# Seven products for eight: the retention values and the first gate by Strassen's scheme

## The chip, the cores and the metric

One core of one Trainium2 chip runs the whole kernel: two blocks of a network on 256 tokens of width 1024, batch 1, all in f32. The metric is the device time of one execution in microseconds. TensorE takes an f32 product as three matmuls of rounded parts, so every weight needs a high and a low part that ScalarE and VectorE make on the fly.

## The reference, cut to what matters

The change lies in the second block, between its first and its second feed-forward layer:

```python
u = rmsnorm(h, norm_mix[l])                       # h: 256 x 1024
proj = u @ w_in[l]
q, k, v, g_ret, p, gates = jnp.split(proj, split_points, axis=-1)
q = rotary(...); k = rotary(...) * (RET_QK_DIM ** -0.5)
ret = retention(q, k, v)                          # scores * inner_decay, then @ v, 4 heads of 256
ret = ret * lax.rsqrt(mean(ret * ret) + NORM_EPS)
ret = ret * jax.nn.silu(g_ret)
pool_out = multiscale_pool(p, pool_w[l], pool_scale[l])
gate = jax.nn.sigmoid(gates.reshape(b, s, 2, D_MODEL) + gate_bias[l])
merged = gate[:, :, 0] * (ret @ w_ret_up[l]) + gate[:, :, 1] * (pool_out @ w_pool_up[l])
h = h + merged @ w_out[l]
```

`v` and the first of the two gates are each a product of u (256 x 1024) with a 1024 x 1024 matrix.

## The kernel before, in words

Five engines run five programs that are written out by hand; each engine executes its list in order, and semaphores join them. A wait stops all that stands behind it on that engine.

**Weights.** They come in units of 1 MB (128 x 2048 f32), one after the other over one DMA queue, into a ring `raw` of four. `hi` (line 206, ScalarE) casts a unit to its high part `whi`, `lo` (line 213, VectorE) writes the rest `wlo`; both rings hold four units as well. `hi` and `lo` of unit v wait until unit v - 4 is used up by TensorE, `lo` waits for `hi`, and the load of unit v waits for `lo` of unit v - 4.

**Products.** `mm3` (line 258) is one f32 product by three matmuls: high x high, high x low, low x high. `quarter` multiplies one half of the input width (j, four slices of 128) for one half of the tokens (t) by one unit: 4 x 3 = 12 matmuls of 512 columns. `chunk` runs the four quarters of 512 output columns, into the PSUM banks 4 and 5. So a unit serves two quarters, 24 matmuls.

**The stage.** TensorE's order in `tensor_ret` (line 2293): pool input p0, p1; second gate g10, g11 with the pool windows between; pool mixing pw; values v0; pool projection pu0, pu1; values v1; q0, k0, q1, k1 with rotation, scores and values of four heads between; retention gate gr0, gr1; first gate g00, g01; retention projection ru0, ru1; output. `scalar_ret` (2393) and `vector_ret` (2464) have the orders of the other two. The names that matter: `vector_gate` (2124) takes a gate out of PSUM with its bias, `scalar_gate` (2136) the sigmoid; `scalar_ret_gate` (2280) empties the banks 4 and 5 of gr0 and gr1 with a SiLU; `vector_ret_norm` (2260) normalises two heads, with two roots on GpSimd in it; `vector_ret_scores` (2224) multiplies scores by the decay mask; `vector_rotary` (2193) rotates q or k; `split_turned_act` / `_dve` (from line 408) make high and low part of a transposed tile; `scalar_pool_out` / `vector_pool_out` (2156, 2164) those of the pool's output. `norm_half_act` (355) and `norm_half_dve` (374) do it for the normalised x of each stage, here the one named `nm`.

## Time and profile before

| | us |
|---|---|
| median of 3 runs | 1196.01 (1195.92 to 1196.31) |
| profiled execution | 1195.67 |
| its span, first to last instruction | 1193.9 |
| TensorE busy (matmul) | 1184.1 |
| VectorE busy | 915.2 |
| ScalarE busy | 674.6 |
| GpSimd busy | 165.2 |

In the profile PE is TensorE's matmuls, PEld its weight loads, which overlap them, DVE is VectorE, ACT is ScalarE, POOL is GpSimd, SP the engine that issues the DMAs. A name such as L218 is a line of the kernel. Many operations go through helpers and so share a line: L218 is `lo`, L211 `hi`, L259 to L261 are the three matmuls of `mm3`, L267 is a transpose.

### The profile page before, as it was taken

The numbers are of one execution on the slowest core, as the hardware profiler recorded it, in microseconds if no ns is written. First come the engines' busy times: TensorE is split into PE (matmuls) and PEld (weight loads), VectorE is DVE, ScalarE is ACT, GpSimd is POOL, SyncE is SP. The second block draws the span as 40 slices with busy tenths as digits, with TensorE's granted clock in tenths as the row PEclk, the third lists the DMA queues.
The fourth block names the chain that finished last, engine by engine and source line by source line (L and its number), as shares of the span: only waits on it lengthen the run. The fifth ranks groups of instructions, "written<-read, shape, count | busy, mean of one in ns | idle before, by whom it ended". The sixth has DMA issues, their size and how long they took to land.

```text
span 1193.9 us, 14696 instructions
## 1 busy us (share of the span) xinstructions
PE 1184.1 (99%) x5728; PEld 982.7 (82%) x5728; DVE 915.2 (77%) x1143; ACT 674.6 (57%) x814; POOL 165.2 (14%) x169
## 2 busy tenths in 40 slices
PE   9999999999999999999999999999999999999997
PEld 8777888888887888888888888888899888888886
DVE  7788898888778798877798878645567666988884
ACT  7775756656646666654666554545333545666552
POOL 2100132210200132210132120000000000222200
PEclk9999999999999999999999999999999999999999
DMA  9434565547333565556455556745544445555540
GB/s 340 177 138 158 183 235 200 183 175 271 129 119 130 187 228 184 187 181 235 149 199 188 182 207 210 281 163 188 201 152 160 158 176 171 189 207 179 189 176 36
DMA packets 32728, 220.91 MB, mean 185 GB/s; under 512 B 3761, under 2 KB 4273, under 8 KB 7058
## 3 DMA queue, kind: packets, MB, share of 16 engines
q1 hardware_dynamic: 32514, 219.77, 51.4%
q8 instruction: 45, 0.74, 0.2%
q14 instruction: 25, 0.20, 0.1%
q10 hardware_dynamic: 144, 0.20, 0.0%
HBM read 218.91 MB, written 1.05 MB: 184 GB/s over the span
## 4 chain that ended last, share of the span: by engine, by line
PE 98%; issue 1%; DVE 1%; ACT 0%; POOL 0%; POOLq 0%; DVEq 0%; ACTq 0%
PE ps L259 30%; PE ps L261 30%; PE ps L260 30%; PE ps L264 5%; PE ps L267 3%; DVE h L406 0%; DVE AR L2579 0%; DVE st L1812 0%; DVE AR L1830 0%; DVE AR L2201 0%; ACT AR L2570 0%; POOLq L134 0%; DVE AR L2202 0%; POOL st L395 0%; POOL state L1546 0%
## 5 line engine op out<-in xcount | busy, mean ns | idle before, releaser
L218 DVE SCALAR_TENSOR_TENSOR wlo<-raw,whi 128x2048 fp32r<-128x2048 f32 x160 | 366.3, 2294 | 116.2 <-ACT whi L211 89.1
L211 ACT CAST whi<-raw 128x2048 fp32r<-128x2048 f32 x162 | 309.9, 1914 | 195.3 <-PE ps L261 193.2
L259 PE MATMUL ps<-whi,xh 128*128 128x512 f32 x1040 | 410.1, 394 | 0.0
L261 PE MATMUL ps<-whi,xl 128*128 128x512 f32 x1040 | 405.4, 390 | 0.0
L260 PE MATMUL ps<-wlo,xh 128*128 128x512 f32 x1040 | 404.9, 389 | 0.0
L259 PEld LDWEIGHTS ps<-whi,xh 128*128 128x128 f32 x1040 | 195.2, 188 | 45.4 <-issue 1.2
L261 PEld LDWEIGHTS ps<-whi,xl 128*128 128x128 f32 x1040 | 195.2, 188 | 42.0
L260 PEld LDWEIGHTS ps<-wlo,xh 128*128 128x128 f32 x1040 | 195.4, 188 | 38.5
L259 PE MATMUL ps<-whi,yh 128*128 128x512 f32 x344 | 137.9, 401 | 0.0
L261 PE MATMUL ps<-whi,yl 128*128 128x512 f32 x344 | 134.4, 391 | 0.0
L260 PE MATMUL ps<-wlo,yh 128*128 128x512 f32 x344 | 134.0, 390 | 0.0
L395 POOL TENSOR_TENSOR st<-st,nhalf 128x1 f32<-128x1 f32 (+3 forms) x28 | 26.8, 959 | 671.4 <-DVE st L386 383.0
L545 ACT ACTIVATE sil<-ps,st 128x256 f32<-128x256 f32 x88 | 42.0, 477 | 123.3 <-PE ps L261 123.3
L243 DVE SCALAR_TENSOR_TENSOR wlo<-raw,whi 128x512 fp32r<-128x512 f32 x152 | 99.4, 697 | 12.5 <-ACT whi L211 11.0
L651 DVE SCALAR_TENSOR_TENSOR hid<-ps,st,sil 128x256 f32<-128x256 f32 x88 | 42.4, 482 | 43.8 <-ACT sil L545 43.8
L261 PEld LDWEIGHTS ps<-whi,yl 128*128 128x128 f32 x344 | 64.6, 188 | 13.7
L831 POOL TENSOR_TENSOR sums<-AR 128x128 f32<-128x128 f32 x32 | 26.7, 836 | 350.4 <-ACT AR L563 350.4
L259 PEld LDWEIGHTS ps<-whi,yh 128*128 128x128 f32 x344 | 64.7, 188 | 12.2 <-issue 0.4
L254 ACT CAST whi<-raw 128x1024 fp32r<-128x1024 f32 x72 | 74.7, 1043 | 0.0
L260 PEld LDWEIGHTS ps<-wlo,yh 128*128 128x128 f32 x344 | 64.8, 188 | 11.8
L836 POOL TENSOR_TENSOR sums<-AR,sums 128x128 f32<-128x128 f32 x32 | 65.0, 2031 | 2.5
L362 ACT ACTIVATE xh<-ps,pr 128x128 fp32r<-128x128 f32 x108 | 29.6, 385 | 47.2 <-PE ps L267 47.2
(256 smaller groups left out, 1381.1 us busy)
## 6 DMA issues: line engine op xcount, KB each, us to landing
raw<-in_w SPq DMA_DIRECT2D x198, 1024.0 KB, 4.8
raw<-in_w SPq DMA_DIRECT2D x4, 512.0 KB, 7.4
h<-in_x SPq DMA_DIRECT2D x4, 256.0 KB, 4.7
raw<-in_w SPq DMA_DIRECT2D x4, 256.0 KB, 4.4
AR<-in_b_pw SPq DMA_DIRECT2D x1, 1024.0 KB, 4.8
AR<-in_gate_bias SPq DMA_DIRECT2D x1, 1024.0 KB, 7.0
AR<-in_dft SPq DMA_DIRECT2D x1, 864.0 KB, 7.7
AR<-in_rmask SPq DMA_DIRECT2D x1, 768.0 KB, 8.9
```

Of the source, the lines that this page charges most:

```text
L211: e.copy(whi[:, v % S, :], raw[:, v % R, :]).then_inc(*sig.up("hi", v))
L218: e.scalar_tensor_tensor(out=wlo[:, v % S, :], in0=raw[:, v % R, :], scalar=1.0, in1=whi[:, v % S, :].bitcast(F32), op0=ALU.mult, op1=ALU. ...
L243: e.scalar_tensor_tensor(out=wlo[:, v % S, cols], in0=raw[:, v % R, cols], scalar=1.0, in1=whi[:, v % S, cols].bitcast(F32), op0=ALU.mult, ...
L254: e.copy(whi[:, v % S, cols], raw[:, v % R, cols]).then_inc(*sig.up("hi", v) if k else sig.up("hi_half", v))
L259: e.matmul(o, ah, bh, start=start, stop=False, skip_group_check=skip)
L260: e.matmul(o, ah, bl, start=False, stop=False, skip_group_check=skip)
L261: return e.matmul(o, al, bh, start=False, stop=stop, skip_group_check=skip)
L264: return e.matmul(o, a, b, start=start, stop=stop, skip_group_check=skip)
L267: return e.transpose(o, i, ident[0:i.shape[0], 0:i.shape[0]])
L545: e.activation(sil[:, t, :], ps[banks.of[key, t]][:, 0:256], ACT.Silu, bias=0.0, scale=rstd[:, t:t + 1]).then_inc(*sig.up("sil", f, j, t))
L651: e.scalar_tensor_tensor(out=hid[:, t, :], in0=ps[b][:, 256:512], scalar=scale, in1=sil[:, t, :], op0=ALU.mult, op1=ALU.mult).then_inc(*ba ...
L836: e.tensor_tensor(s4, a12, s2, ALU.subtract).then_inc(*sig.up("sums", f, j))
```

## The change

Both `v` and the first gate are computed as one group each, in place of two chunks. The input is cut into four blocks (two token halves x two width halves), the weight matrix into four of 512 x 512 by width half and output half: b11, b21, b12, b22, each a unit. Seven block products of 12 matmuls, four on sums of weight blocks, give the result, where the eight quarters were. In detail:

- `tensor_product` runs product p = 0 to 6 of a group with weight unit v + p, each unit for one product. Products 0, 2 and 5 take x itself, the other four take sums of x blocks (`sxh`, `sxl`) that are made once for both groups. The order in TensorE's queue: v0 and v1 become one group between pw and pu0, so v1 moves ahead of pu0, pu1. The group g0 stands where g00, g01 stood, with the transposes of the second half after products 1 and 2.
- Four of the seven units are sums of weight blocks. `vector_group_sum` makes each in place in the `raw` ring, 128x2048 f32 on VectorE: sum 1 (b11 + b12) after `lo` of unit v, sum 6 (b12 + b22), sum 4 (b22 + sum 1) after `lo` of v + 3, sum 5 (b21 + sum 4) after `lo` of v + 2. `hi` of these units waits for the sum. A group is loaded as four units and split as seven, so the loads of later units wait for the last user of a buffer.
- The result is put together by `scalar_part` (four copies out of PSUM, scaled, on ScalarE) and `vector_part` (four scaled additions on VectorE). The first gate's bias is added by four `vector_gate_sum`.
- The banks of a group are 4, 5 and 6 for v, 4, 5 and 2 for g0. The second product takes bank 5.
- x of this stage is kept in f32 (`x32`): ScalarE writes x32 out of PSUM, copies it to the high part, VectorE subtracts. Four sums on VectorE, one copy on ScalarE and one subtraction give `sxh`, `sxl`.
- `vector_ret_scores` of heads 0 and 1 moves ahead of the rotation of q1's first half and the `lo` behind it.
- The size of a scratch area for DMA descriptors is set to 8192.

```diff
@@ -26,7 +26,11 @@
+         "ffa": 33, "ret": 47, "ffb": 33}
+RET = {"p0": 2, "p1": 2, "g10": 2, "g11": 2, "pw": 1, "v": 7, "pu0": 2, "pu1": 2, "q0": 2, "k0": 2, "q1": 2, "k1": 2,
+       "gr0": 2, "gr1": 2, "g0": 7, "ru0": 2, "ru1": 2, "out": 4}
+GROUPS = ("v", "g0")
+GROUP_RAW = (0, 0, 2, 1, 1, 2, 3)
...
+        raw_of, n = [], 0
+        while len(raw_of) < NU:
+            if len(raw_of) in (RU[g] for g in GROUPS):
+                raw_of += [n + k for k in GROUP_RAW]
+                n += 4
+            else:
+                raw_of.append(n)
+                n += 1
+        users = {}
+        for v, n in enumerate(raw_of):
+            users.setdefault(n, []).append(v)
+        sums_at = {RU[g] + k: RU[g] for g in GROUPS for k in (1, 4, 5, 6)}
...
+            if name == "nm":
+                b = banks.of["x", name, t, half]
+                q.wait_ge(*sig.at("sums", "n1", FAST - 1))
+                q.wait_ge(*sig.at("turned_lo", "n1", FAST - 1))
+                for i in range(4):
+                    k = 4 * half + i
+                    last = e.activation(x32[:, t, k, :], ps[b][:, 128 * i:128 * i + 128], ACT.Copy, bias=0.0,
+                                        scale=parm(name, k))
+                last.then_inc(*banks.empty("x", name, t, half))
+                q.wait_ge(*banks.emptied("x", name, t, half))
+                if x_free:
+                    q.wait_ge(*x_free)
+                e.copy(xh[:, 4 * half:4 * half + 4, tcols(t)],
+                       x32[:, t, 4 * half:4 * half + 4, :]).then_inc(*sig.up("xh", name, t, half))
+                return
...
+            if name == "nm":
+                at = (slice(None), slice(4 * half, 4 * half + 4), tcols(t))
+                e.tensor_tensor(xl[at], x32[:, t, 4 * half:4 * half + 4, :], xh[at].bitcast(F32),
+                                ALU.subtract).then_inc(*sig.up("x_low", t, half))
+                return
...
+        GBANK = {"v": (4, 5, 6), "g0": (4, 5, 2), "g1": (4, 5, 2)}
+        DONE = {(0, 0): "y0", (0, 1): "z", (1, 0): "y1", (1, 1): "x"}
...
+        def vector_group_sum(e, q, g, k):
+            v = RU[g]
+            b11, b21, b22, b12 = (raw_at(v + i) for i in (0, 2, 3, 6))
+            if k == 1:
+                q.wait_ge(*lo_at(v))
+                q.wait_ge(*sig.at("raw%d" % (raw_of[v + 6] % R), raw_of[v + 6]))
+                d = e.tensor_tensor(b11, b11, b12, ALU.add)
+            elif k == 6:
+                q.wait_ge(*sig.at("summed", v + 1))
+                q.wait_ge(*sig.at("raw%d" % (raw_of[v + 3] % R), raw_of[v + 3]))
+                d = e.tensor_tensor(b12, b12, b22, ALU.add)
+            elif k == 4:
+                q.wait_ge(*lo_at(v + 3))
+                q.wait_ge(*sig.at("summed", v + 6))
+                d = e.tensor_tensor(b22, b22, b11, ALU.add)
+            else:
+                q.wait_ge(*lo_at(v + 2))
+                q.wait_ge(*sig.at("summed", v + 4))
+                d = e.tensor_tensor(b21, b21, b22, ALU.add)
+            d.then_inc(*sig.up("summed", v + k))
+
+        def tensor_product(e, q, g, p):
+            bx, bz, by = GBANK[g]
+            v = RU[g] + p
+            b, key = ((bx, "x"), (bz, "z"), (by, "y0"), (bz, None), (bx, None), (by, "y1"), (bx, None))[p]
+            if key:
+                banks.take(b, g, key)
+                q.wait_ge(*banks.room(g, key))
+            else:
+                q.wait_ge(*sig.at("part", g, {3: 1, 4: 0, 6: 2}[p]))
+            if p in (0, 2, 5):
+                t, half = {0: (0, 0), 2: (0, 1), 5: (1, 1)}[p]
+                q.wait_ge(*x_low(t, half))
+                ah, al = (y[:, 4 * half:4 * half + 4, tcols(t)] for y in (xh, xl))
+            else:
+                t, half = {1: (1, 1), 3: (0, 1), 4: (0, 0), 6: (1, 0)}[p]
+                q.wait_ge(*sig.at("x_low", "sums"))
+                ah, al = (y[:, t, 4 * half:4 * half + 4, :] for y in (sxh, sxl))
+            q.wait_ge(*lo_at(v))
+            for k in range(4):
+                c = slice(512 * k, 512 * k + 512)
+                last = mm3(e, ps[b][:, :], ah[:, k, :], al[:, k, :], whi[:, v % S, c], wlo[:, v % S, c],
+                           k == 0 and key is not None, k == 3, skip=True)
+            last.then_inc(*sig.up("made", g, p))
+            sig.alias("used", (v,), "made", (g, p))
+
+        def scalar_part(e, q, g, i):
+            bx, bz, _ = GBANK[g]
+            p, b, t, j = ((0, bx, 0, 0), (1, bz, 1, 1), (4, bx, 0, 1), (6, bx, 1, 0))[i]
+            q.wait_ge(*sig.at("made", g, p))
+            q.wait_ge(*sig.at("summed", "minus"))
+            q.wait_ge(*(banks.filled("sc", 3) if g == "g0" else banks.filled("pooled", 3)))
+            e.activation(group_dst(g, t, j), ps[b][:, :], ACT.Copy, bias=0.0,
+                         scale=(minus if j else rstd)[:, t:t + 1]).then_inc(*sig.up("part", g, i))
+
+        def vector_part(e, q, g, i):
+            bx, bz, by = GBANK[g]
+            p, b, t, j, parts = ((2, by, 0, 0, (0,)), (3, bz, 0, 1, (2,)), (6, bx, 1, 1, (1, 3)), (5, by, 1, 0, (3,)))[i]
+            q.wait_ge(*sig.at("made", g, p))
+            for n in parts:
+                q.wait_ge(*sig.at("part", g, n))
+            d = group_dst(g, t, j)
+            e.scalar_tensor_tensor(out=d, in0=ps[b][:, :], scalar=(minus if j else rstd)[:, t:t + 1], in1=d, op0=ALU.mult,
+                                   op1=ALU.add).then_inc(*banks.empty(g, DONE[t, j]))
+
...
+            e.copy(sxh, x32).then_inc(*sig.up("xh", "sums"))
+
+        def vector_token_sums_low(e, q):
+            q.wait_ge(*sig.at("xh", "sums"))
+            e.tensor_tensor(sxl, x32, sxh.bitcast(F32), ALU.subtract).then_inc(*sig.up("x_low", "sums"))
 
...
+        def vector_gate_sum(e, q, which, j, t):
+            g = group_dst(f"g{which}", t, j)
+            q.wait_ge(*group_done(f"g{which}", j, t))
+            q.wait_ge(*sig.at("ld_gb", 0))
+            e.tensor_tensor(g, g, gb[:, 1024 * which + 512 * j:1024 * which + 512 * j + 512],
+                            ALU.add).then_inc(*sig.up("summed", "gate", which, j, t))
...
             sig.alias("used", (u,), "full3", ("pw", 3))
-            chunk(e, q, "v0", RU["v0"], x)
+            for p in range(7):
+                tensor_product(e, q, "v", p)
             chunk(e, q, "pu0", RU["pu0"], y_pool, (0, 1), yh, yl)
             chunk(e, q, "pu1", RU["pu1"], y_pool, (0, 1), yh, yl)
             sig.alias("y_free", ("pool",), "full1", ("pu1", 1))
-            chunk(e, q, "v1", RU["v1"], x)
...
-            for half, key in enumerate(("gr1", "g00")):
-                quarter(e, q, key, RU[key], 0, 0, 4, xh, xl, x)
-                quarter(e, q, key, RU[key], 0, 1, 4, xh, xl, x)
-                turn_x(e, q, "ret", None, 0, half, vn[:, 0, :], "y", sig.at("gated", half, 0))
-                quarter(e, q, key, RU[key], 1, 0, 5, xh, xl, x)
-                turn_x(e, q, "ret", None, 1, half, vn[:, 1, :], "y", sig.at("gated", half, 1))
-                quarter(e, q, key, RU[key], 1, 1, 5, xh, xl, x)
-            chunk(e, q, "g01", RU["g01"], x)
-            sig.alias("x_free", ("nm",), "full5", ("g01", 1))
+            quarter(e, q, "gr1", RU["gr1"], 0, 0, 4, xh, xl, x)
+            quarter(e, q, "gr1", RU["gr1"], 0, 1, 4, xh, xl, x)
+            turn_x(e, q, "ret", None, 0, 0, vn[:, 0, :], "y", sig.at("gated", 0, 0))
+            quarter(e, q, "gr1", RU["gr1"], 1, 0, 5, xh, xl, x)
+            turn_x(e, q, "ret", None, 1, 0, vn[:, 1, :], "y", sig.at("gated", 0, 1))
+            quarter(e, q, "gr1", RU["gr1"], 1, 1, 5, xh, xl, x)
+            for p in range(7):
+                tensor_product(e, q, "g0", p)
+                if p in (1, 2):
+                    turn_x(e, q, "ret", None, p - 1, 1, vn[:, p - 1, :], "y", sig.at("gated", 1, p - 1))
+            sig.alias("x_free", ("nm",), "made", ("g0", 6))
...
-            scalar_pool_out(e, q)
+            scalar_pool_out(e, q, (0, 1, 2))
             hi(e, q, RU["pw"] + 4)
-            for t in range(2):
-                scalar_copied(e, q, "v0", 0, t)
-                hi(e, q, RU["v0"] + 4 + t)
+            scalar_pool_out(e, q, (3,))
+            scalar_part(e, q, "v", 0)
+            scalar_part(e, q, "v", 1)
+            hi(e, q, RU["v"] + 4)
+            hi(e, q, RU["v"] + 5)
+            hi(e, q, RU["v"] + 6)
+            scalar_part(e, q, "v", 2)
+            hi(e, q, RU["v"] + 7)
+            hi(e, q, RU["v"] + 8)
+            scalar_part(e, q, "v", 3)
+            hi(e, q, RU["v"] + 9)
+            hi(e, q, RU["v"] + 10)
...
+            scalar_part(e, q, "g0", 0)
+            scalar_part(e, q, "g0", 1)
+            hi(e, q, RU["g0"] + 4)
+            split_turned_act(e, q, "y", "ret", 0, 1, yh)
+            hi(e, q, RU["g0"] + 5)
+            split_turned_act(e, q, "y", "ret", 1, 1, yh)
+            hi(e, q, RU["g0"] + 6)
+            hi(e, q, RU["g0"] + 7)
+            scalar_part(e, q, "g0", 2)
+            hi(e, q, RU["g0"] + 8)
+            scalar_part(e, q, "g0", 3)
+            hi(e, q, RU["g0"] + 9)
             scalar_gate(e, q, 0, 0, 0)
-            split_turned_act(e, q, "y", "ret", 0, 1, yh)
-            hi(e, q, RU["g00"] + 4)
-            split_turned_act(e, q, "y", "ret", 1, 1, yh)
+            hi(e, q, RU["g0"] + 10)
             scalar_gate(e, q, 0, 0, 1)
-            hi(e, q, RU["g00"] + 5)
             for t in range(2):
...
+            lo(e, q, RU["p0"] + 4)
+            lo(e, q, RU["p0"] + 5)
+            vector_minus(e, q)
+            vector_token_sums(e, q)
+            lo(e, q, RU["p1"] + 4)
+            lo(e, q, RU["p1"] + 5)
+            vector_token_sums_low(e, q)
...
-            for t in range(2):
-                vector_gate(e, q, 1, 1, t)
-                lo(e, q, RU["g11"] + 4 + t)
-            vector_pool_out(e, q)
-            lo(e, q, RU["pw"] + 4)
-            lo(e, q, RU["v0"] + 4)
-            lo(e, q, RU["v0"] + 5)
+            vector_gate(e, q, 1, 1, 0)
+            vector_group_sum(e, q, "v", 1)
+            lo(e, q, RU["v"] + 1)
+            vector_gate(e, q, 1, 1, 1)
+            vector_group_sum(e, q, "v", 6)
+            lo(e, q, RU["v"] + 2)
+            vector_pool_out(e, q, (0, 1, 2))
+            lo(e, q, RU["v"] + 3)
+            vector_group_sum(e, q, "v", 4)
+            vector_group_sum(e, q, "v", 5)
+            lo(e, q, RU["v"] + 4)
+            vector_part(e, q, "v", 0)
+            lo(e, q, RU["v"] + 5)
+            lo(e, q, RU["v"] + 6)
+            vector_pool_out(e, q, (3,))
+            vector_part(e, q, "v", 1)
+            lo(e, q, RU["v"] + 7)
+            vector_part(e, q, "v", 2)
+            vector_part(e, q, "v", 3)
+            lo(e, q, RU["v"] + 8)
+            lo(e, q, RU["v"] + 9)
+            lo(e, q, RU["v"] + 10)
...
+            vector_ret_scores(e, q, 0)
+            vector_ret_scores(e, q, 1)
             vector_rotary(e, q, "q1", 0)
             lo(e, q, RU["q1"] + 4)
-            vector_ret_scores(e, q, 0)
-            vector_ret_scores(e, q, 1)
...
             vector_ret_norm(e, q, 1)
-            lo(e, q, RU["gr0"] + 5)
+            vector_group_sum(e, q, "g0", 1)
+            lo(e, q, RU["g0"] + 1)
             vector_ret_gate(e, q, 1, 0)
             split_turned_dve(e, q, "y", "ret", 0, 0, yh, yl)
-            lo(e, q, RU["gr1"] + 4)
+            vector_group_sum(e, q, "g0", 6)
+            lo(e, q, RU["g0"] + 2)
             split_turned_dve(e, q, "y", "ret", 1, 0, yh, yl)
             vector_ret_gate(e, q, 1, 1)
-            lo(e, q, RU["gr1"] + 5)
-            vector_gate(e, q, 0, 0, 0)
+            lo(e, q, RU["g0"] + 3)
+            vector_group_sum(e, q, "g0", 4)
+            vector_group_sum(e, q, "g0", 5)
             split_turned_dve(e, q, "y", "ret", 0, 1, yh, yl)
-            lo(e, q, RU["g00"] + 4)
+            lo(e, q, RU["g0"] + 4)
             split_turned_dve(e, q, "y", "ret", 1, 1, yh, yl)
-            vector_gate(e, q, 0, 0, 1)
-            lo(e, q, RU["g00"] + 5)
-            for t in range(2):
-                vector_gate(e, q, 0, 1, t)
-                lo(e, q, RU["g01"] + 4 + t)
+            vector_part(e, q, "g0", 0)
+            lo(e, q, RU["g0"] + 5)
+            lo(e, q, RU["g0"] + 6)
+            vector_part(e, q, "g0", 1)
+            lo(e, q, RU["g0"] + 7)
+            vector_gate_sum(e, q, 0, 0, 0)
+            vector_part(e, q, "g0", 2)
+            vector_part(e, q, "g0", 3)
+            lo(e, q, RU["g0"] + 8)
+            vector_gate_sum(e, q, 0, 0, 1)
+            vector_gate_sum(e, q, 0, 1, 0)
+            vector_gate_sum(e, q, 0, 1, 1)
+            lo(e, q, RU["g0"] + 9)
+            lo(e, q, RU["g0"] + 10)
...
-                q.wait_ge(*lo_at(v - R))
+                q.wait_ge(*raw_free(v - R))
                 load(raw[:, v % R, :], wst[v], "raw%d" % (v % R), v)
```

## Rows read from the trace of the kernel before

**Rows 1.** The page: busy time of each engine, share of the span, instructions.

```profile
PE 1184.1 (99%) x5728; PEld 982.7 (82%) x5728; DVE 915.2 (77%) x1143; ACT 674.6 (57%) x814; POOL 165.2 (14%) x169
```

**Rows 2.** TensorE's waits over the kernel: total, times, longest, in us.

```profile
PE ps L264 <- POOL state L1546: 1.4, 1, 1.4
PE ps L264 <- DVE AR L2233: 0.9, 1, 0.9
PE ps L267 <- DVE AR L1830: 0.6, 1, 0.6
PE ps L264 <- ACT yh L1862: 0.6, 1, 0.6
```

**Rows 3.** Timeline of TensorE: start us, duration us, engine, line, operation, idle before.

```profile
813.71 0.40 PE L259 MATMUL ps<-whi,xh 128*128 128x512 f32 x1
...
824.62 0.39 PE L259 MATMUL ps<-whi,yh 128*128 128x512 f32 x1
...
894.30 0.28 PE L261 MATMUL ps<-xh,wlo 128*128 128x256 f32 x1
895.50 0.67 PE L264 MATMUL ps<-AR 128*128 128x256 f32 x2 [0.91 <-DVE AR L2233]
```

**Rows 4.** Busy us by stage: length, PE, PEld, DVE, ACT, POOL, clock, DMA.

```profile
801.50:824.60 23.10, 23.10 (x126) 20.09 (x125) 12.99 (x15) 12.28 (x15) 0.00 (x0) 1.00 0.53 183
937.70:960.40 22.70, 22.70 (x105) 18.80 (x104) 13.09 (x12) 12.16 (x11) 0.00 (x0) 1.00 0.58 202
```

**Rows 5.** VectorE groups by shape: busy us, mean ns of one, idle before.

```profile
L218 DVE SCALAR_TENSOR_TENSOR wlo<-raw,whi 128x2048 fp32r<-128x2048 f32 x160 | 366.3, 2294 | 116.2 <-ACT whi L211 89.1 <-ACT whi L254 27.1
L684 DVE TENSOR_TENSOR raw<-raw 128x512 f32<-128x512 f32 x32 | 22.2, 693 | 1.1
L2579 DVE TENSOR_TENSOR AR<-h,AR 128x1024 f32<-128x1024 f32 x1 | 1.2, 1226 | 0.1
L2132 DVE SCALAR_TENSOR_TENSOR AR<-ps,st,AR 128x512 f32<-128x512 f32 x8 | 6.0, 746 | 2.1 <-PE ps L261 2.0
```

**Rows 6.** ScalarE groups by shape: busy us, mean ns, idle before.

```profile
L211 ACT CAST whi<-raw 128x2048 fp32r<-128x2048 f32 x162 | 309.9, 1914 | 195.3 <-PE ps L261 193.2 <-DMA raw<-in_w 0.5
L2121 ACT ACTIVATE AR<-ps,st 128x512 f32<-128x512 f32 x8 | 5.6, 696 | 11.3 <-PE ps L261 11.3
```

**Rows 7.** Timeline of VectorE, then ScalarE, ahead of the values.

```profile
802.72 0.75 DVE L2132 SCALAR_TENSOR_TENSOR AR<-ps,st,AR 128x512 f32<-128x512 f32 x1
807.43 2.29 DVE L218 SCALAR_TENSOR_TENSOR wlo<-raw,whi 128x2048 fp32r<-128x2048 f32 x1 [3.96 <-ACT whi L211]
809.64 0.74 DVE L2132 SCALAR_TENSOR_TENSOR AR<-ps,st,AR 128x512 f32<-128x512 f32 x1
...
815.08 3.22 DVE L2168 SCALAR_TENSOR_TENSOR yl<-ps,pr,yh 128x256 fp32r<-128x256 f32 x8
...
810.96 1.88 ACT L211 CAST whi<-raw 128x2048 fp32r<-128x2048 f32 x1
```

**Rows 8.** Timeline of VectorE, ScalarE and TensorE ahead of the first gate.

```profile
932.79 2.29 DVE L218 SCALAR_TENSOR_TENSOR wlo<-raw,whi 128x2048 fp32r<-128x2048 f32 x1
...
937.90 0.69 ACT L2285 ACTIVATE AR<-ps,st 128x512 f32<-128x512 f32 x1 [0.76 <-PE ps L261]
...
937.70 0.39 PE L259 MATMUL ps<-whi,xh 128*128 128x512 f32 x1
...
943.15 0.60 PE L267 MATMUL ps<-kc,AR 128*128 128x128 f32 x4
943.50 0.48 PE L259 MATMUL ps<-whi,xh 128*128 128x512 f32 x1
```

**Rows 9.** Timeline of ScalarE and VectorE behind the norm's first token half.

```profile
758.15 1.96 ACT L211 CAST whi<-raw 128x2048 fp32r<-128x2048 f32 x1
...
760.15 2.29 DVE L218 SCALAR_TENSOR_TENSOR wlo<-raw,whi 128x2048 fp32r<-128x2048 f32 x1 [0.44 <-ACT whi L211]
```

**Rows 10.** DMA issues: operation, KB each, median us to landing.

```profile
raw<-in_w SPq DMA_DIRECT2D x41, 1024.0 KB, 4.8
```

126 lines of the change are left out of this document (78 added, 48 removed).

## Prediction

> **What bounds the kernel now.** I read first the busy line of the page [rows 1]: TensorE is busy for 1184.1 of the 1193.9 us of the span. The list of its waits [rows 2] has only four entries, 3.5 us together. So TensorE's program is the time: a matmul that goes is a gain, unless TensorE then has to wait. Its pitch comes from the timeline [rows 3]: the first product chunk of the values starts at 813.71 and the next chunk at 824.62, with 48 matmuls of 512 columns between, so 0.227 us each (the 0.39 us of a record overlaps its neighbours), and 2.73 us for a block product of 12. The table by stage [rows 4] shows what the other engines do beside it: in the stage that ends with the values' first half VectorE is busy for 13.0 of 23.1 us, in that of the first gate for 13.1 of 22.7 us. That is the spare time which the change wants to use, some 10 us in each.
>
> **TensorE's saving.** Values and first gate lose one product of eight each: 2 x 2.73 = 5.46 us. Nothing else leaves TensorE's queue.
>
> **What VectorE gets for it.** Per group: three more weight units to be split, so three more low parts of 2.29 us and three more high parts of 1.91 us on ScalarE [rows 5, 6]; four sums of 128x2048 f32. The trace has no such sum. It has the same addition on 512 columns at 0.693 us and on 1024 at 1.226 us [rows 5], so 1.04 us per 1000 columns and 2.29 us for 2048; below it could be no more than the 1.9 us of ScalarE's 2048-wide copy, above it 2.45 us if reading and writing one buffer disturbs something. I take 2.28, next to the low part of the same width. Then there are four combinations out of PSUM of 0.75 us, like the gate's [rows 5]; for the first gate four additions of 0.69 us besides, in place of the four gate instructions. A group therefore adds 3 x 2.29 + 4 x 2.28 + 3 = 19 us to VectorE in a stage of 19.1 us (7 x 2.73) in which it was already busy for over half. VectorE does not fit beside the group. What is left is how much of it lies ahead of the group, in its queue's order, and how late it makes each product. An independent instruction starts about 0.08 us before the one ahead of it ends (807.43 + 2.29 against 809.64 [rows 7]); one that depends starts 0.03 us after it. With that I walk the queues.
>
> The Trainium skill, "VectorE: DVE Perf Modes", section "The perf-mode tier table", puts the fp32 two-tensor operation in the slowest tier, at 2293 ns for 2048 elements. No row here shows that instruction; by that figure the sum below would be the same to 0.1 us.
>
> **The values (v), in the clock of the trace before.** VectorE meets the first half-gate at 802.72 [rows 7]. Then: sum 1 803.4 to 805.65; ScalarE casts unit v+1 until 807.6; low v+1 until 809.9; second half-gate; sum 6 810.5 to 812.8; low v+2 813.1 (its cast ends then, behind a sigmoid, as in [rows 7], where the cast of that turn starts 810.96) to 815.4; six of the eight pool instructions, 2.4 us (the eight took 3.22 [rows 7]), to 817.7; low v+3 to 819.95; sum 4 to 822.2; sum 5 to 824.5; the cast of v+4 could start only after sum 4 and is done at 824.2; low v+4 824.4 to 826.7. From 807.6 on VectorE rests for 0.4 us in 19. TensorE needs v+4 for its fifth product at 813.71 + 4 x 2.73 = 824.6: it waits 2.1 us. Low v+5 ends 829.6 (0.1 us late) and v+6 is in time; the seventh product ends 835.0. The pool projection pu0 needs its first weights, low part done 835.4: 0.4 us late. Its second unit stands in VectorE's queue behind two combinations that wait for the seventh product: 0.07 + 0.69 (ScalarE's part) + 0.07 + 0.68 + 0.68 + 2.29 = 4.5 us after that product, while TensorE comes for it after 2.7: these two waits are 1.8 us together, of which I counted 0.4 already, so 1.4 more. Sum of waits 2.1 + 0.1 + 1.8 = 4.0; less the product saved 2.73: **+1.3 us**. The raw weights are not late: a load lands 4.8 us after its issue [rows 10], and that of pu0's second unit, released by low v+4 at 826.7, is there at 831.6, ahead of its cast at 832.
>
> **Mask products ahead of a rotation.** TensorE waited 0.91 us at 895.50 for them [rows 3], queued behind a rotation and a low part. Now they run as soon as the scores are there (890.6 to 892.4), well before TensorE's last q product ends at 894.4, and the rotation that goes behind them frees its bank at 893.6, needed at 897. **-0.95 us**, and nothing is next in line.
>
> **The norm's x as f32 copy.** Each half of x gets one more copy on ScalarE (0.6 us and its wait), twice ahead of the cast of [rows 9] (758.15 becomes 759.5); the low part behind it (760.15 becomes 761.5) then ends 763.8, and the x of the second token half is ready at 764.45 against TensorE's 764.35: **+0.15 us**. The token sums (four of 0.7 us, one high copy, one low part of 2.3) lie between 775 and 788, where VectorE idles for 5 us, and delay nothing that TensorE asks for.
>
> **The first gate (g0).** VectorE's last instruction before it ends its slot at 932.79 [rows 8]. Sum 1 to 935.1. The cast of g0+1, ahead in ScalarE's queue of the retention gate that frees bank 4 and of the one that frees bank 5, waits for it: 935.1 to 937.0. Bank 4 is free at 937.6, just in time for product 1 at 937.7 [rows 8]; bank 5, after the cast of g0+2, a turned copy and the last gate, at 941.0, where product 2 wants it at 940.4: 0.7 late (before, that gate started at 937.90 [rows 8]). VectorE without a pause from 937.05: low g0+1, gate, turned copy, sum 6, low g0+2 until 944.96. TensorE is there at 944.2 (941.1 + 2.73, and 0.35 for the transposes, [rows 8]): 0.8 late. Turned copy, gate, low g0+3 until 948.4: 0.25 late. Sum 4 950.7, sum 5 953.0, turned copy, low g0+4 953.7 to 956.0, where TensorE comes at 951.2: **4.8 late**. Turned copy, combination, low g0+5 until 959.5 against 958.8: 0.75. g0+6 is in time, the seventh product ends 965.0. Then, as in v, 1.8 for the second unit of ru0 behind the combinations. Waits 0.7 + 0.8 + 0.25 + 4.8 + 0.75 + 1.8 = 9.1; less 2.73: **+6.4 us**. From ru0 on the old pattern is met again and TensorE has no slack to give anything back.
>
> **Sum.** 1.3 - 0.95 + 0.15 + 6.4 = 6.9 us. The profiled execution took 1195.67 us (span 1193.9 and 1.8 around it); 1202.6 with the change. The median of the three runs is 0.34 above the profiled one, so **1202.9 us**. The unsure terms: sums at 1.9 or 2.45 us move low g0+4 by 3 x 0.38 = 1.1 earlier or 0.5 later, low v+4 likewise: -2.2 and +1.0. The pauses between dependent instructions may be 0.1 longer at some ten places: +1. An order that I read wrongly in one of the two stages could give back its largest wait: -2.1 or -4.8. So 1197.5 to 1205 for this case.
>
> **The rivals.** (1) VectorE keeps up after all: the spare 10 us of each stage [rows 4] and the four-unit ring take the work, as the low part of the fifth unit is made in time. Then both products are gained, and the wait of [rows 2]: -5.46 - 0.95, **1189.6**. For it: the mean load of VectorE over the kernel is 77% [rows 1], and it rests for most of the stage before the values. Against: the sums can't start before the last low part of their first block and the loaded second block, and the queue holds them behind the half-gate of 802.7 and the retention norm of 932.8. The point where it decides is the fifth product. (2) Only the values or only the gate stalls; a group at its gain of 2.73 and the other as above: with the gate clean -2.73 + 1.3 - 0.8 = -2.2, **1193.8**; with a half of the gate's waits 1198.3, within or near no change. For it: a walk of 13 dependent steps. (3) Clock: everything here ran at the upper level, 2.4 GHz (granted 1.00 in both stages [rows 4]), and no wait of TensorE was longer than 1.4 us [rows 2]. If the gap of 4.8 us lowers it to 1.2 GHz, the product behind the gap takes 5.5 in place of 2.7 us; 0.75 of that is covered by the wait that follows, and a second slow product could follow: +2 to +4, **1206**. No row prices it. The Trainium skill, "TensorE: Matmul & The Clock Gate", section "Why this matters for your kernels", says that gaps of TensorE between bursts of matmuls bring the half rate back; no run here shows it yet. (4) The change does not cut the matmuls as it says: the loop over seven products of 12 leaves no doubt, 24 matmuls fewer; no chance.
>
> **How the numbers follow.** Forecast (stalls in both groups, most in the gate) 0.68; clock lowered besides 0.12; one stage clean or half clean 0.12; all clean 0.08. Range 1196.5 to 1207: it leaves out rival 1, the faster half of rival 2 and the far end of rival 3. A measurement can tell about 0.2%, 2.4 us: faster (below 1193.6) gets rival 1 and a little of rival 2, 0.10; within it the rest of rival 2 and the near tail of the forecast, 0.11; slower 0.79.
>
> **What would show it.** In the profile after: 24 fewer matmuls of 512 columns; the wait on the mask products gone; in the list of waits new entries of TensorE on the low part, the longest about 4.8 us before the fifth product of the gate, 2.1 before that of the values, some 13 us together; VectorE busy without a pause from 807 to 840 and from 937 to 970. Wrong would be: no wait at the fifth products (then the queue's order or the cost of a sum is other than I took it), a wait on loads of raw weights, or a granted clock below 1.00 behind the long gap.

## The result and the profile after

The kernel after takes **1208.48 us** (1206.91 to 1209.31) against 1195.92 for the kernel before on the same chip: ratio 1.0100, 95% interval 1.0089 to 1.0112. The profiled execution took 1207.04, its span is 1205.3 us, 11.4 more than before. The forecast was 1202.9, range up to 1207.0: the direction came, the size was almost twice what I had worked out, and the time lies above the range.

The busy line of the page of the kernel after, and the clock of TensorE in 40 slices of the span; the first answers to [rows 1]:

```profile
PE 1184.5 (98%) x5704; PEld 980.7 (81%) x5704; DVE 954.4 (79%) x1159; ACT 691.8 (57%) x829; POOL 165.2 (14%) x169
PEclk9999999999999999999999999999999899999999
```

TensorE runs 24 matmuls fewer, 5704 in place of 5728, and yet is busy for 0.4 us more. So 5.5 us of matmuls went and came back in another form; the one slice with an 8 in the clock row says which.

TensorE's waits over the kernel after, which answers to [rows 2]:

```profile
PE ps L293 <- DVE wlo L252: 10.7, 5, 4.6
PE ps L298 <- POOL state L1600: 1.4, 1, 1.4
PE ps L298 <- ACT whi L262: 0.9, 1, 0.9
PE ps L301 <- DVE AR L1884: 0.6, 1, 0.6
PE ps L298 <- ACT yh L1916: 0.6, 1, 0.6
PE ps L293 <- ACT AR L2445: 0.3, 1, 0.3
```

The mask wait of 0.9 us is gone. Five waits on a low part (L252 is `lo` of the kernel after) came, 10.7 us. The wait on L262 lies at the very start of the kernel, on the first weights. It differs from execution to execution (none to 1.4 us in the kernels below) and is no part of the change. The product behind it begins at 6.83 us, in the kernel before at 6.31, and the stage begins 0.36 us later (754.83 and 754.47). The other profiles mostly pair late with late as well (6.38 and 754.42, 6.91 and 755.19, 7.12 and 755.08), so the 0.36 is put down to the start of the run.

The timeline of TensorE in the kernel after, with the first matmul of most products of the values, and of the fifth product of each group all that show its pace; it answers to [rows 3] and [rows 8] (SX is the high part of a sum of x blocks, sxl its low part):

```profile
814.19 0.40 PE L293 MATMUL ps<-whi,xh 128*128 128x512 f32 x1
...
816.94 0.40 PE L293 MATMUL ps<-whi,SX 128*128 128x512 f32 x1
...
819.74 0.39 PE L293 MATMUL ps<-whi,xh 128*128 128x512 f32 x1
...
822.49 0.40 PE L293 MATMUL ps<-whi,SX 128*128 128x512 f32 x1
...
827.34 0.50 PE L293 MATMUL ps<-whi,SX 128*128 128x512 f32 x1 [1.89 <-DVE wlo L252]
827.67 0.53 PE L294 MATMUL ps<-wlo,SX 128*128 128x512 f32 x1
827.99 0.63 PE L295 MATMUL ps<-whi,sxl 128*128 128x512 f32 x1
...
830.98 0.50 PE L293 MATMUL ps<-whi,SX 128*128 128x512 f32 x1
...
831.77 0.39 PE L293 MATMUL ps<-whi,xh 128*128 128x512 f32 x1
...
842.03 0.47 PE L293 MATMUL ps<-whi,yh 128*128 128x512 f32 x1 [1.83 <-DVE wlo L252]
...
958.86 0.79 PE L293 MATMUL ps<-whi,SX 128*128 128x512 f32 x1 [4.55 <-DVE wlo L252]
959.45 0.63 PE L294 MATMUL ps<-wlo,SX 128*128 128x512 f32 x1
959.88 0.63 PE L295 MATMUL ps<-whi,sxl 128*128 128x512 f32 x1
...
964.14 0.48 PE L293 MATMUL ps<-whi,xh 128*128 128x512 f32 x1
...
974.53 0.47 PE L293 MATMUL ps<-whi,yh 128*128 128x512 f32 x1 [1.84 <-DVE wlo L252]
```

The fifth product of the values runs from 827.34 to 831.77, 4.43 us, and that of the gate from 958.86 to 964.14, 5.28 us, where 2.73 was the price. Their matmuls are 0.43 us apart (959.45 to 959.88) in place of 0.227, with records of 0.63 in place of 0.39 us. The table by stretch names the cause; its columns are those of [rows 4], the granted clock ahead of the last two numbers:

```profile
827.00:828.00 1.00, 0.67 (x3) 0.52 (x4) 1.00 (x3) 1.00 (x2) 0.00 (x0) 0.89 0.01 0
828.00:831.00 3.00, 3.00 (x9) 2.35 (x8) 3.00 (x2) 0.82 (x1) 0.00 (x0) 0.50 0.93 303
836.00:846.00 10.00, 8.16 (x37) 6.39 (x36) 8.51 (x6) 4.54 (x4) 0.00 (x0) 1.00 0.67 238
957.00:958.00 1.00, 0.00 (x0) 0.00 (x0) 1.00 (x1) 1.00 (x2) 0.00 (x0) 0.74 0.63 262
958.00:964.00 6.00, 5.14 (x12) 4.08 (x13) 6.00 (x5) 3.79 (x3) 0.00 (x0) 0.50 0.63 194
964.00:966.00 2.00, 2.00 (x9) 1.60 (x9) 1.28 (x3) 1.62 (x2) 0.00 (x0) 0.92 0.93 393
```

Behind both long waits the granted clock is 0.50, which is the 1.2 GHz level, and comes back to 1.00 only about when the product ends. Around 842 and 974, where TensorE waited 1.8 us, it stayed at 1.00. A busy TensorE is therefore not a TensorE at work: the two slow products add 4.25 us of busy time.

Position by position, the kernel after against the one before: stage entered +0.36 us (the start of the run); norm +0.12 (values begin at 814.19, before at 813.71); values +3.44 (the first q product begins at 861.18, before at 857.26); masks -1.14 (the next q or k product behind the scores at 900.75, before at 897.97); first gate +8.74 (a later block of eight transposes at 1000.12, before at 988.60); at the end of the span +11.4.

### The profile page after: what moved, and what is told of

It is laid out like the page before. It is cut to its first block, busy times and chain, and to the rows that moved or that the text cites. A ratio compares the mean times of both kernels' runs of the same rounds, so it can differ in the third digit from the quotient of the medians.

```text
span 1205.3 us, 14698 instructions
## 1 busy us (share of the span) xinstructions
PE 1184.5 (98%) x5704; PEld 980.7 (81%) x5704; DVE 954.4 (79%) x1159; ACT 691.8 (57%) x829; POOL 165.2 (14%) x169
## 4 chain that ended last, share of the span: by engine, by line
PE 93%; DVE 4%; issue 2%; ACT 1%; DMA 0%; POOL 0%; SPq 0%; POOLq 0%; DVEq 0%; ACTq 0%
PE ps L293 29%; PE ps L295 28%; PE ps L294 28%; PE ps L298 5%; PE ps L301 3%; DVE wlo L252 1%; ACT whi L245 1%; DVE raw L2170 0%; DVE raw L2162 0%; DMA raw<-in_w 0%; DVE AR L2218 0%; POOL st L449 0%; DVE yl L2327 0%; DVE st L2429 0%; ACT AR L2208 0%
## 5 line engine op out<-in xcount | busy, mean ns | idle before, releaser
L252 DVE SCALAR_TENSOR_TENSOR wlo<-raw,whi 128x2048 fp32r<-128x2048 f32 x166 | 379.7, 2294 | 84.5 <-ACT whi L245 57.3
L245 ACT CAST whi<-raw 128x2048 fp32r<-128x2048 f32 x168 | 321.0, 1914 | 202.7 <-PE ps L295 183.0
L293 PE MATMUL ps<-whi,xh 128*128 128x512 f32 x1000 | 394.7, 395 | 0.6 <-DVE wlo L252 0.6
L295 PE MATMUL ps<-whi,xl 128*128 128x512 f32 x1000 | 390.0, 390 | 0.0
L294 PE MATMUL ps<-wlo,xh 128*128 128x512 f32 x1000 | 389.8, 390 | 0.0
L293 PEld LDWEIGHTS ps<-whi,xh 128*128 128x128 f32 x1000 | 187.9, 188 | 45.2 <-issue 2.0
L295 PEld LDWEIGHTS ps<-whi,xl 128*128 128x128 f32 x1000 | 187.8, 188 | 40.2
L294 PEld LDWEIGHTS ps<-wlo,xh 128*128 128x128 f32 x1000 | 188.1, 188 | 36.7
L752 DVE TENSOR_TENSOR FS<-AR,FS 128x1536 fp32r<-128x1536 f32 x32 | 56.1, 1752 | 0.0
```

The source lines that it names most:

```text
L245: e.copy(whi[:, v % S, :], raw_at(v)).then_inc(*sig.up("hi", v))
L252: e.scalar_tensor_tensor(out=wlo[:, v % S, :], in0=raw_at(v), scalar=1.0, in1=whi[:, v % S, :].bitcast(F32), op0=ALU.mult, op1=ALU.subtrac ...
L293: e.matmul(o, ah, bh, start=start, stop=False, skip_group_check=skip)
L294: e.matmul(o, ah, bl, start=False, stop=False, skip_group_check=skip)
L295: return e.matmul(o, al, bh, start=False, stop=stop, skip_group_check=skip)
L752: e.tensor_tensor(mixl, mix, mixh.bitcast(F32), ALU.subtract).then_inc(*sig.up("mixed_lo", v))
```

## The experiments

All medians are beside runs of the kernel before on the same chip (1195.9 to 1196.1), and the ratios are against those. A difference between two changed kernels is a difference of their medians; the medians of the kernel before that stand beside them lie within 0.15 us of each other.

**1. Only the masks.** The kernel before, with `vector_ret_scores` of heads 0 and 1 ahead of the rotation and nothing else:

```diff
-            vector_rotary(e, q, "q1", 0)
-            lo(e, q, RU["q1"] + 4)
             vector_ret_scores(e, q, 0)
             vector_ret_scores(e, q, 1)
+            vector_rotary(e, q, "q1", 0)
+            lo(e, q, RU["q1"] + 4)
```

> The kernel before with one edit: the mask products of heads 0 and 1 ahead of the rotation of q1's first half. My account says that TensorE's wait of 0.9 us for them goes and that nothing takes its place: 1.1 us less than before, as the distance between the first q product and the first k1 product shrank by 1.1 us in the changed kernel, so about 1194.8. The rival says that the rotation put behind them is now what TensorE meets: no change, 1195.9.

1194.77 us against 1196.07, ratio 0.9990 (0.9981 to 0.9999). The wait on the mask products is out of the list, and the profiled execution's span is 1192.8, so 1.1 shorter. This part of the change is a gain of its own, of 0.1%: the interval only just leaves 1 out.

**2. The gap filled.** The kernel after, with matmuls on parts of x whose results nobody reads, 8 ahead of the fifth product of the values and 19 ahead of that of the gate, into idle PSUM banks. TensorE's gaps are taken away, while every wait on VectorE ends when it did:

```diff
+FILL = {"v": 8, "g0": 19}
...
+            if p == 4:
+                for n in range(FILL[g]):
+                    mm(e, ps[7 if g == "v" else 0][:, :], xh[:, 0, 0:P], xh[:, 0:2, :], skip=True)
```

> The changed kernel; ahead of the fifth product of each group TensorE runs matmuls whose result nobody reads, 8 in the values and 19 in the first gate, in place of idling for 2 and 4.6 us. My account says that the gap in TensorE's work is what lowers the clock: the granted clock stays 1.00 in both places, the two products behind the gaps take 2.7 us in place of 4.4 and 5.3, and the time falls by some 3.8 us to about 1204.5, although more is computed. The rival says that the low clock belongs to this stretch for another reason (a management of power, the products on token sums): then the fifth products are still slow and the time stays at 1208 or rises.

1204.08 us, ratio 1.0070 (1.0057 to 1.0082): **4.4 us faster than the kernel after by doing more**. The waits, then the first matmul of the gate's fifth product, then the table by stretch over both fifth products:

```profile
PE ps L294 <- DVE wlo L253: 4.7, 5, 1.8
```

```profile
957.17 0.50 PE L294 MATMUL ps<-whi,SX 128*128 128x512 f32 x1 [0.25 <-DVE wlo L253]
```

```profile
824.00:830.00 6.00, 5.95 (x26) 4.34 (x24) 6.00 (x5) 4.06 (x3) 0.00 (x0) 1.00 0.74 266
952.00:961.00 9.00, 8.27 (x35) 6.22 (x34) 8.85 (x7) 8.80 (x7) 0.00 (x0) 1.00 0.64 227
```

The clock is 1.00 in both stretches. The low parts come when they came before; only the half clock is gone. That isolates it as the cause of some 4 us. The 8 us that are left above the kernel before come from the lateness of the low parts: 4.7 us of waits as printed, and the time that TensorE now spends on the unread matmuls in place of idling, less what the change saves.

**3. Sums of 8 columns.** The same instructions, with the eight sums cut to 128x8, so the weights of four products in each group are not the sums:

```diff
-                d = e.tensor_tensor(b11, b11, b12, ALU.add)
+                d = e.tensor_tensor(b11[:, 0:8], b11[:, 0:8], b12[:, 0:8], ALU.add)
```

> The changed kernel, with the eight sums of weight blocks cut down to 8 of 2048 columns: this part of the computation is left out. My account says that the sums on VectorE (2.28 us each) are what makes the fifth products late: without them VectorE is 6.6 us ahead there, both long waits go, the clock stays up, and what is left is 1.8 us of waits behind the combinations in each group: 1193 to 1195. The rival says that the extra casts and low parts in order are enough to hold TensorE up: then waits of several us stay at the fifth products, 1200 or more.

1195.24 us, ratio 0.9996 (0.9987 to 1.0005). The waits on the low part:

```profile
PE ps L293 <- DVE wlo L252: 4.1, 3, 1.8
```

Both long waits are gone, the clock stayed at 1.00, and the rest is the wait at the second unit of pu0 and of ru0 (1.79 and 1.84 us) and one of 0.49. So the eight sums, 18.3 us of VectorE, cost 13.2 us of kernel time. That it is their place in the queue and not their work shows in experiment 6, which keeps all eight.

**4. The low part ahead of the combinations.** `lo` of the second unit behind each group is moved ahead of the two `vector_part` that wait for the seventh product:

```diff
+            lo(e, q, RU["v"] + 8)
             vector_part(e, q, "v", 2)
             vector_part(e, q, "v", 3)
-            lo(e, q, RU["v"] + 8)
```

> The changed kernel; the low part of the unit that follows a group by two goes ahead of the last two combinations in VectorE's queue, in both groups. My account says that the two waits of 1.8 us at the second units of the pool and the retention projection go, 3.5 us less: about 1205. The rival says that the wait only moves, as the combinations are then late for the gate's additions, the banks or the loads: 1208.

1201.61 us, ratio 1.0045 (1.0033 to 1.0058), so 6.9 less than the kernel after where 3.5 was expected.

```profile
PE ps L293 <- DVE wlo L252: 7.0, 3, 4.6
```

The waits of 1.83 and 1.84 us are gone, as foretold. In the profiles it is 5.4 us (span 1199.9 against 1205.3): 3.7 of waits, about 0.6 of restarts behind them, and 0.8 because the gate's slow product took 4.44 in place of 5.28 us with the same gap ahead of it (4.56). So a like gap doesn't cost the same each time. Cut by single microseconds, the profiles show the difference: in the kernel after the granted clock was already down to 0.74 at 957 to 958, about a microsecond before the product began (958.86); here it was 1.00 until 957 and 0.54 at 957 to 958, and the product had begun at 956.36 with its first matmuls at full pace. The further 1.5 us between the medians is likely the clock too: its mean was 0.995 to 0.997 in this kernel's executions and 0.993 to 0.995 in those of the kernel after; no profile shows where.

**5. One sum earlier besides.** The kernel of 4, with the gate's sum 1 ahead of the second retention norm. In the kernel after VectorE idles for 1.90 us ahead of that norm, for ScalarE (L2414), and for 1.98 us behind the sum, for the cast that waits for it:

```diff
-            vector_ret_norm(e, q, 1)
             vector_group_sum(e, q, "g0", 1)
+            vector_ret_norm(e, q, 1)
```

> The kernel of e4_lo_first, and in the first gate's group sum 1 goes ahead of the retention norm in VectorE's queue, into the time in which VectorE waits for the scores' product. My account says that the sum and ScalarE's wait for it (2.2 + 2.0 us) leave the chain that makes the gate's fifth product late: that wait falls from 4.6 to about 2.6 us, the short ones on bank 5 and on the third product (0.3 and 0.6 us) go, and the time falls by about 3 us to 1198.7. If the clock needs a longer gap than what is left, 2 us more. The rival says that the chain is bound by its low parts and casts after the norm: the wait stays near 4.6 us, 1201.6.

1197.11 us (1196.05 to 1199.95), ratio 1.0010 (1.0002 to 1.0019): one line moved, 4.5 us less than experiment 4, where 3 was expected (the wait fell to 2.22 us, 2.6 was expected). In the profile the sum runs from 924.70 to 926.98 and the norm begins at 926.90 without a pause: the sum costs VectorE nothing there. The two waits on low parts that are left:

```profile
827.71 0.50 PE L293 MATMUL ps<-whi,SX 128*128 128x512 f32 x1 [1.89 <-DVE wlo L252]
...
951.99 0.50 PE L293 MATMUL ps<-whi,SX 128*128 128x512 f32 x1 [2.22 <-DVE wlo L252]
```

The first is the very wait of the kernel after, 1.89 us before the same product. Here the product took 2.95 us and kept its clock; there it took 4.43. Behind the second the pitch went to 0.43 us after six matmuls, and the product took 4.21.

**6. The groups reordered.** No instruction added or taken away, nothing cut. Sum 1 of the gate ahead of the norm, sum 6 behind the low part v+2, what nobody waits for yet (pool output, turned copies, gate sums) behind the low parts of the fifth to ninth units, and the cast of v+2 ahead of a sigmoid on ScalarE. The two orders for the values on VectorE:

```diff
-            vector_group_sum(e, q, "v", 6)
             lo(e, q, RU["v"] + 2)
-            vector_pool_out(e, q, (0, 1, 2))
+            vector_group_sum(e, q, "v", 6)
             lo(e, q, RU["v"] + 3)
...
             lo(e, q, RU["v"] + 6)
-            vector_pool_out(e, q, (3,))
-            vector_part(e, q, "v", 1)
+            vector_pool_out(e, q, (0, 1))
             lo(e, q, RU["v"] + 7)
+            vector_pool_out(e, q, (2, 3))
+            lo(e, q, RU["v"] + 8)
+            vector_part(e, q, "v", 1)
```

> The changed kernel with both groups' orders rewritten on VectorE and ScalarE, no work added or left out: casts ahead of the sigmoid and the pool's parts, the low parts that TensorE wants next ahead of all that can wait. Walking the queues gives waits of TensorE of about 1.6 us in the values and 2.4 us in the gate: 1196.0 - 5.5 - 1.1 + 0.1 + 4.0 = 1193.5, and 1195.3 if the clock falls once. The rival says that VectorE's work for a group does not fit in any order: 1198 or more.

**1194.05 us**, ratio 0.9986 (0.9977 to 0.9995), 14.4 us under the kernel after with the same work.

```profile
PE ps L293 <- DVE wlo L252: 2.5, 4, 1.4
```

**7. One sum on GpSimd.** The kernel of 6, with sum 6 of both groups on GpSimd, which is idle there. It is not quite the kernel of 6 otherwise: in the values three parts of the pool's output stand ahead of the low part v+3 on VectorE again (`vector_pool_out(e, q, (0, 1, 2))`, 2.43 us), and the fourth behind that of v+7.

```diff
             lo(e, q, RU["v"] + 2)
-            vector_group_sum(e, q, "v", 6)
...
         def gpsimd_ret(e, q):
             norm_pool(e, q, "nm", 1)
+            vector_group_sum(e, q, "v", 6)
```

> The kernel of e6_reordered, with sum 6 of each group on GpSimd, which idles in this stage, and not on VectorE. GpSimd's addition of 512 columns took 1.85 us, so one of 2048 some 7.4 us, and it has 12 us from sum 1 to sum 4 in the values and 10 in the gate. VectorE is 2.3 us ahead at the fifth products: waits of 0.3 us in the values and under 1.5 us in the gate, no fall of the clock: 1191.3. The rival says that GpSimd's work slows VectorE's in the same stretch or is late for sum 4: 1194 or more.

1199.45 us, ratio 1.0025 (1.0017 to 1.0034), 5.4 slower than without, where 2.8 faster was expected; the rival held. The timelines of GpSimd and of VectorE around the first and the second of these sums:

```profile
806.34 4.63 POOL L2168 TENSOR_TENSOR raw<-raw 128x2048 f32<-128x2048 f32 x1 [39.01 <-DVE raw L2164]
...
808.24 4.89 DVE L254 SCALAR_TENSOR_TENSOR wlo<-raw,whi 128x2048 fp32r<-128x2048 f32 x1 [1.98 <-ACT whi L247]
...
931.98 4.62 POOL L2168 TENSOR_TENSOR raw<-raw 128x2048 f32<-128x2048 f32 x1
...
932.05 5.10 DVE L2435 TENSOR_TENSOR AR<-AR,st 128x512 f32<-128x512 f32 x1 [0.81 <-POOL st L451]
```

GpSimd ends at 810.97, VectorE's 2.29 us operation that began beside it at 813.13, so 2.16 after it; in the second case GpSimd ends at 936.60 and VectorE's 0.69 us operation at 937.15. VectorE stood still until GpSimd was done, both times. That agrees with the Trainium skill, "SBUF — State Buffer", section "Who interferes with whom", by which a VectorE operation with two inputs from SBUF and a GpSimd operation that reads SBUF exclude each other, and the later one waits for the whole of the other. GpSimd's two sums took the same, 4.63 and 4.62 us (the estimate was 7.4), though VectorE came 1.90 us into the first and 0.07 us into the second; no run has such a sum with VectorE at rest beside it. TensorE then waited 2.12 us (product 2.96) and 2.77 us (product 4.45, half clock), where in the kernel of 6 it waited 0.15 and 1.37. The pool's parts did not make the first of them: low v+3 starts at 818.48, right behind its cast on ScalarE (816.50 to 818.44), and that cast stood behind a sigmoid and pool parts that waited for the half-gate which VectorE could finish only at 813.79, behind the stopped operation (in the kernel of 6 at 811.32).

**8. The gap alone.** The kernel before, with two waits of TensorE on GpSimd put into the chunks v1 and g01; none of the change's work is in it:

```diff
+GAP = {"v1": 5, "g01": 12}
...
             for t in range(2):
+                if key in GAP and t == 1:
+                    q.wait_ge(*sig.at("gap", key))
```

> The kernel before, with two idle gaps of TensorE put in and nothing else: about 2 us in the middle of the values' second chunk and about 4.7 us in the middle of the first gate's second chunk, where TensorE waits for small clears on GpSimd. My account of the clock says that a gap alone lowers it: after the gap of 4.7 us the twelve matmuls that follow take about 5 us in place of 2.7, and after that of 2 us they may. Time: 1196.0 + 6.7 + 2 to 4 = 1205 to 1207. The rival says that the slow products of the changed kernel had another reason: the matmuls behind both gaps keep 0.227 us each, 1202.7.

1205.71 us, ratio 1.0081 (1.0068 to 1.0095). Waits, the matmul behind the second gap, and the table by stretch there:

```profile
PE ps L261 <- POOL rest L2556: 6.5, 2, 4.5
```

```profile
962.13 0.74 PE L261 MATMUL ps<-whi,xh 128*128 128x512 f32 x1 [4.49 <-POOL rest L2556]
```

```profile
961.00:962.00 1.00, 0.00 (x0) 0.00 (x0) 0.00 (x0) 0.00 (x0) 0.83 (x4) 1.00 0.80 336
962.00:964.00 2.00, 1.87 (x5) 1.49 (x6) 0.00 (x0) 0.00 (x0) 0.07 (x1) 0.55 0.69 291
964.00:966.00 2.00, 2.00 (x7) 1.57 (x6) 0.00 (x0) 0.00 (x0) 0.00 (x0) 0.59 0.00 0
966.00:968.00 2.00, 2.00 (x11) 1.64 (x10) 0.00 (x0) 1.17 (x1) 0.00 (x0) 1.00 0.00 0
```

A gap does it without any sum, ring or Strassen product: behind 4.49 us the next 24 matmuls took 7.17 us (962.13 to 969.30) in place of 5.46. Behind the gap of 2.00 us the clock stayed.

**9. A second round of the same.** The kernel of 6, with sum 6 of the values moved on into VectorE's idle 2 us ahead of the cast, two parts of the pool's output in its old place, and in the gate's group a split and a gate operation behind the low parts of units five to seven. TensorE's transposes of what that gate operation makes move from behind the third product to behind the seventh (p = 2 and 6 in the code, which counts from 0; the expectation calls them the second and the sixth):

```diff
-                if p in (1, 2):
+                if p in (1, 6):
...
             vector_group_sum(e, q, "v", 1)
+            vector_group_sum(e, q, "v", 6)
             lo(e, q, RU["v"] + 1)
...
-            split_turned_dve(e, q, "y", "ret", 1, 0, yh, yl)
-            vector_ret_gate(e, q, 1, 1)
             lo(e, q, RU["g0"] + 3)
             vector_group_sum(e, q, "g0", 4)
             vector_group_sum(e, q, "g0", 5)
...
+            split_turned_dve(e, q, "y", "ret", 1, 0, yh, yl)
+            vector_ret_gate(e, q, 1, 1)
             lo(e, q, RU["g0"] + 7)
```

> The reordered kernel with a second round of moves, no work added or taken away: the sixth product's sum of the values stands right behind the first's, in VectorE's idle time ahead of the cast it waits for, and in the gate's group one split and one gate operation stand behind the low parts of the fifth to seventh units, with TensorE's transpose of that head moved from behind the second product to behind the sixth. Theory (what was left of TensorE's waits there, 0.15, 0.20, 0.77 and 1.37 us, is only VectorE's order): they go, with about 0.2 us of restart each, so 1.1 to 3 us under the reordered kernel's 1194.1: about 1191.5. Rival (VectorE has no slack left over these stretches, so what is taken from ahead of one low part turns up ahead of another, at the gate's second half): waits of the same sum in other places, 1194 or more.

The kernel of 6 once more beside it:

> The reordered kernel once more, on the chip of the second round of moves, so that the two can be compared: 1194.0 to 1194.3, 0.9986 of the kernel before.

**1192.70 us** (1192.07 to 1192.88), ratio 0.9972 (0.9961 to 0.9982); beside it the kernel of 6 took 1194.08, ratio 0.9984 (0.9975 to 0.9993).

```profile
PE ps L293 <- DVE wlo L252: 1.1, 3, 0.6
```

The theory holds: the waits went from 2.5 to 1.1 us and the time by 1.4, with no new wait at ru0. It gave less than the 2.6 I hoped for, since 0.15, 0.33 and 0.65 us of waits are left. This is the fastest version of the change, 15.8 us under the kernel after and 2.1 under the masks alone (experiment 1). So of the 5.5 us of matmuls that the change saves it keeps about 2; the kernel of 6, 0.7 under the masks alone with overlapping intervals, is not shown to keep any.

## Why the prediction was right and wrong

- **Bound, saving, sums: right.** TensorE's program was the time. A product of x takes 2.75 us (819.74 to 822.49), one of a sum of x 2.80 (816.94 to 819.74). The price of a sum, taken as 2.28 between bounds of 1.9 and 2.45 (the upper one a guess, as no row had it), was 2.28 to 2.29. That is also the Trainium skill's figure on "VectorE: DVE Perf Modes", section "The perf-mode tier table" (2293 ns): here trace and page agree.
- **The walk of the queues: right to a few tenths.** VectorE in the kernel after, ahead of the values' fifth product, and ahead of the gate:

```profile
803.87 2.28 DVE L2162 TENSOR_TENSOR raw<-raw 128x2048 f32<-128x2048 f32 x1
808.13 2.29 DVE L252 SCALAR_TENSOR_TENSOR wlo<-raw,whi 128x2048 fp32r<-128x2048 f32 x1 [1.98 <-ACT whi L245]
...
822.78 2.29 DVE L2174 TENSOR_TENSOR raw<-raw 128x2048 f32<-128x2048 f32 x1
824.99 2.29 DVE L252 SCALAR_TENSOR_TENSOR wlo<-raw,whi 128x2048 fp32r<-128x2048 f32 x1
...
934.96 0.69 DVE L2433 TENSOR_TENSOR AR<-AR,st 128x512 f32<-128x512 f32 x1 [0.81 <-POOL st L449]
935.57 2.28 DVE L2162 TENSOR_TENSOR raw<-raw 128x2048 f32<-128x2048 f32 x1
...
956.52 2.28 DVE L252 SCALAR_TENSOR_TENSOR wlo<-raw,whi 128x2048 fp32r<-128x2048 f32 x1
```

 With the 0.48 us by which the values began later, low v+4 was forecast at 824.9 and stands at 824.99. Its wait was 1.89 (forecast 2.1), those behind the combinations 1.83 and 1.84 (1.8 each), the long one 4.55 (4.8), the second and third of the gate 0.34 (0.7) and 0.58 (0.8). The 0.75 at the gate's sixth product, and the 0.25 at its fourth, did not show; the sixth was swallowed by the slow fifth (in experiment 2, where the fifth keeps its clock, TensorE waits 0.48 there). Waits together 3.72 + 7.31 = 11.0 against 13.1.
- **Masks and norm: right.** -1.14 and +0.12 against -0.95 and +0.15 (the prediction's own positions for the norm, 764.45 and 764.35, give 0.10); experiment 1 gives -1.3 alone.
- **The failed step: the clock stood among the rivals, with a chance of 0.12, and not in the sum.** The prediction had a gap of 4.8 us in its own walk and gave it no price in the sum: no row ahead of it showed a longer wait than 1.4 us, so none had the price. A missing row was treated as a price of zero. It had named a granted clock below 1.00 behind the long gap as a sign of being wrong, and that sign came. The terms are 1.70 us in the values (4.43 less 2.73) and 2.55 in the gate (5.28 less 2.73), 4.25 together: just above that rival's +2 to +4, and it came in both groups, where the rival had only the gap of 4.8. Experiment 2 takes it away (-4.4), experiment 8 makes one such fall in the kernel before.
- **A term that was missing: the restart.** A wait costs more than the idle time that the profile prints. Between 822.49 and 827.34 lie 4.85 us, a product of 2.80 and 1.89 of idle time, and 0.16 more; the pipelined record ends 0.16 us after the next one could have begun. Behind the wait the first matmul is followed after 0.33 us (827.67) in place of 0.23, and a product that kept its clock took 2.95 or 2.96 in place of 2.80 (experiments 5, 7). That is 0.25 to 0.3 us for each of four waits and 0.16 for the two ahead of the slow products, whose first matmul is counted with the clock. With the 0.07 us by which each of the other six products on sums is slower it makes some 1.8 us. What the account below needs is more, 0.75 in the values and 1.6 in the gate: these two are what is left over there, not measured terms. Of the difference 0.2 us stands behind the second pair of transposes in the gate, where the next product begins after 0.57 us (950.70 to 951.27) in place of 0.35; why is not shown.
- **The account.** Values: -2.73 + 3.72 + 1.70 + 0.75 = 3.44. Gate: -2.73 + 7.31 + 2.55 + 1.6 = 8.73. Against the forecast 4.25 and 2.3 came on top, 0.36 from the start of the run, and 2.1 of waits and 0.2 of masks less than thought: +4.6, which is 11.4 less 6.9 to about 0.1. Between profile and median lies another 1 us: executions whose mean granted clock was 0.995, the profiled one among them, took 1206.9 and 1207.0, those with 0.993 1208.5 to 1209.3.
- **The range** took the size of a sum, pauses and misread orders in, but the two terms that only add time had no part in it. The forecast's own upper end of 1205 with the clock rival's 4 us on top would have reached 1209, above the measured time. The lower end of 1197.5 does not follow from the terms listed: the largest, 4.8 us off 1202.9, gives 1198.1.
- **The rival "VectorE keeps up"** fell for this order of the queue only. Its point of decision was named rightly (the fifth product), and the orders of experiments 6 and 9 meet most of it: with 2.5 and 1.1 us of waits left they come to 1194.05 and 1192.70; its full gain was 1189.6.

## What to carry to other kernels

Where an engine program is full, price a wait of TensorE as its idle time plus a restart of 0.25 to 0.3 us, and from about 2 us of idle time on put the loss of the clock (here 1.4 to 2.6 us for each) into the range, at 4.5 us into the sum. Work that trades matmuls for vector work should first be placed in the other engine's order by due time: the same instructions gave 1208.5 and 1192.7 us here. Before a wait is taken as the price of a change, ask what stands ahead of the late operation in its queue that nobody needs yet.
